# Weight units split in two halves by GpSimd, tensor tiles that wait half by half, four rows at the end of the first tiles, and two convolutions in another order

## The reference

```python
for l in range(2):
    x = layer_norm(ALPHA * x + 0.5 * swiglu(x, ffn_w12[l, 0], ffn_w3[l, 0]), ...)
    x = layer_norm(ALPHA * x + hybrid_mixer(x, ...), ...)          # delta net, RG-LRU, band attention
    x = layer_norm(ALPHA * x + memory_cross_attention(x, mem, xa_wq[l], xa_wkv[l], xa_wo[l]), ...)
    x = layer_norm(ALPHA * x + 0.5 * swiglu(x, ffn_w12[l, 1], ffn_w3[l, 1]), ...)
```

## Time and profile before

| | us |
|---|---|
| median of 3 runs | 3212.9 |
| lowest and highest run | 3211.45, 3213.68 |
| time of the profiled execution | 3213.97 |
| its span, first to last instruction | 3212.1 |
| PE busy | 3122.7 (97%) |
| POOL busy | 1751.3 (55%) |
| DVE busy | 1485.7 (46%) |
| ACT busy | 713.5 (22%) |

### The profile page before, as it was taken

How to read it: one execution, slowest core, us unless ns; L and a number is a source line. 1 busy time by engine, 2 the same in 40 slices (tenths; PEclk the granted TensorE clock), 3 DMA queues, 4 the chain that set the end, 5 groups by cost and what they waited for, 6 DMA issues and landing times.

```text
span 3212.1 us, 44735 instructions
## 1 busy us (share of the span) xinstructions
PE 3122.7 (97%) x15968; PEld 2598.2 (81%) x15968; DVE 1485.7 (46%) x2218; ACT 713.5 (22%) x1433; POOL 1751.3 (55%) x1003
## 2 busy tenths in 40 slices
PE   8999999999999999999999999999999999999997
PEld 7888876788888878888888888667888888788886
DVE  4342357755536335332243314667565372353423
ACT  1110223422222223110121102244222122231102
POOL 6666553433346755666656675525333558466663
PEclk9999999999999999999999999999999999999998
DMA  4233221211122322323323233212111223222231
GB/s 152 93 98 104 97 92 40 73 56 57 53 79 86 112 79 86 98 94 102 99 87 98 98 100 101 79 47 73 53 53 54 91 86 119 72 86 97 93 104 60
DMA packets 81190, 272.94 MB, mean 85 GB/s; under 512 B 8432, under 2 KB 16912, under 8 KB 81040
## 3 DMA queue, kind: packets, MB, share of 16 engines
q1 hardware_dynamic: 75808, 264.27, 25.3%
q10 hardware_dynamic: 5088, 5.96, 0.6%
q0 software_dynamic: 144, 0.66, 0.1%
HBM read 268.73 MB, written 2.12 MB: 84 GB/s over the span
## 4 chain that ended last, share of the span: by engine, by line
PE 88%; DVE 4%; issue 4%; POOL 2%; ACT 1%; DMA 0%; DVEq 0%; ACTq 0%; POOLq 0%; SPq 0%
PE acc L613 76%; PE aux L613 11%; POOL wh L596 1%; POOL wl L598 1%; PE aux L874 1%; DVE ycl L1720 0%; DVE dc L1891 0%; ACT xf L1317 0%; DVE li L1950 0%; DVE xl L1720 0%; DVE xf L1799 0%; DVE lc L1951 0%; DMA raw<-in_stream 0%; ACT tmp L1317 0%; ACT xh L1317 0%
## 5 line engine op out<-in xcount | busy, mean ns | idle before, releaser
L596 POOL TENSOR_SCALAR wh<-raw 128x1024 fp32r<-128x1024 f32 x496 | 540.2, 1089 | 1378.9 <-PE acc L613 792.1
L598 POOL TENSOR_TENSOR wl<-raw,wh 128x1024 fp32r<-128x1024 f32 x496 | 1212.4, 2444 | 41.3
L613 PE MATMUL acc<-xh,wh 128*128 128x512 f32 (+1 forms) x2688 | 1016.2, 383 | 32.3 <-ACT xh L1317 14.7
L613 PE MATMUL acc<-xh,wl 128*128 128x512 f32 (+1 forms) x2688 | 986.4, 372 | 0.0
L613 PE MATMUL acc<-xl,wh 128*128 128x512 f32 (+1 forms) x2688 | 942.4, 372 | 0.0
L613 PEld LDWEIGHTS acc<-xh,wh 128*128 128x128 f32 x2688 | 514.3, 191 | 142.3 <-issue 39.4
L613 PEld LDWEIGHTS acc<-xh,wl 128*128 128x128 f32 x2688 | 514.6, 191 | 79.1 <-issue 1.9
L613 PEld LDWEIGHTS acc<-xl,wh 128*128 128x128 f32 x2688 | 487.1, 191 | 87.4
L1720 DVE TENSOR_TENSOR hl<-tmp,hh 128x512 f32 x88 | 236.9, 2692 | 81.9 <-ACT hh L1317 81.9
L613 PE MATMUL acc<-hl,wh 128*128 128x512 f32 (+1 forms) x704 | 264.5, 376 | 0.0
L613 PE MATMUL acc<-hh,wl 128*128 128x512 f32 (+1 forms) x704 | 264.5, 376 | 0.0
(11 more groups left out here) (286 smaller groups left out, 3924.1 us busy)
## 6 DMA issues: line engine op xcount, KB each, us to landing
raw<-in_stream SPq DMA_DIRECT2D x496, 512.0 KB, 3.3
xf<-in_xT SPq DMA_DIRECT2D x2, 1024.0 KB, 9.6
bias<-rel_scratch ACTq DMA_DIRECT2D x2, 1024.0 KB, 6.0
mraw<-in_memT ACTq DMA_DIRECT2D x2, 1024.0 KB, 6.0
out_xT<-xf SPq DMA_DIRECT2D x16, 128.0 KB, 1.7
gate_w<-in_gate_w ACTq DMA_DIRECT2D x2, 512.0 KB, 4.8
const<-in_const POOLq DMA_DIRECT2D x1, 640.0 KB, 7.4
sc<-in_ba_w ACTq DMA_DIRECT2D x2, 256.0 KB, 4.9
```

The lines of the kernel that those rows point to most:

```text
L596: pool.tensor_scalar(wh[:, s, :], raw[:, s, :], 1.0, 0.0, ALU.mult, ALU.add).then_inc(hi_step, 1)
L598: pool.tensor_tensor(wl[:, s, :], raw[:, s, :], wh[:, s, :].bitcast(F32), ALU.subtract).then_inc(unit_split, 1)
L613: return pe.matmul(out, w, x, start=start, stop=stop, skip_group_check=True)
```

## The change

1. **Halves.** `split` does a unit in two halves of 512 columns: high part, remainder, high part, remainder. `unit_split` and `hi_step` now count halves. SyncE's wait is doubled accordingly.
2. **Waits half by half.** `simple_tile` and `first_pairs` wait for the first half of the unit ahead of k = 0, and for the second ahead of k = 4. Every other user of a unit waits for both halves, as before.
3. **Four rows at the end.** `together` is `KD // 2` = 4 where it was 6.
4. **Start.** The transfers of the two halves of x are issued one unit later each.
5. **Banks.** `att_v` and `mem_v` wait for a bank ahead of that bank's first matmul.
6. **Convolutions.** For head 0, conv2 moves from level 2 behind `rate` in level 4; conv1 of head 1 moves from there behind silu2 in level 5.
7. **Merge.** `low_part` of the two earlier rows stands ahead of the drain of the next two.

```diff
@@ def dve_beside
-            2: only(n, "decay", "silu0", "conv2"), 4: [(n - 1, "rate")] + (only(1, "conv1") if n == 0 else []),
-            5: only(n, "k_normed", "silu2") + only(p, "z_gate"), 6: only(p, "o_normed", "y") + only(n, "q_normed")}.get(s, [])
+            2: only(n, "decay", "silu0") + (only(n, "conv2") if n else []),
+            4: [(n - 1, "rate")] + (only(0, "conv2") if n == 0 else []),
+            5: only(n, "k_normed", "silu2") + (only(1, "conv1") if n == 0 else []) + only(p, "z_gate"),
+            6: only(p, "o_normed", "y") + only(n, "q_normed")}.get(s, [])
...
@@ SyncE
-                if s < 2:
-                    sp.dma_start(xf[:, :, tokens(s)], x_rows[:, :, tokens(s)]).then_inc(x_loaded[s], 16)
+                if 1 <= s < 3:
+                    sp.dma_start(xf[:, :, tokens(s - 1)], x_rows[:, :, tokens(s - 1)]).then_inc(x_loaded[s - 1], 16)
...
-                    sp.wait_ge(unit_split, i * SLOTS + (s - SLOTS + 1))
+                    sp.wait_ge(unit_split, i * (2 * SLOTS) + 2 * (s - SLOTS + 1))
...
@@ GpSimd
             def split(i, s):
-                pool.tensor_scalar(wh[:, s, :], raw[:, s, :], 1.0, 0.0, ALU.mult, ALU.add).then_inc(hi_step, 1)
-                pool.wait_ge(hi_step, i * SLOTS + (s + 1))
-                pool.tensor_tensor(wl[:, s, :], raw[:, s, :], wh[:, s, :].bitcast(F32), ALU.subtract).then_inc(unit_split, 1)
+                for m in range(2):
+                    c = slice(m * UNIT // 2, (m + 1) * UNIT // 2)
+                    pool.tensor_scalar(wh[:, s, c], raw[:, s, c], 1.0, 0.0, ALU.mult, ALU.add).then_inc(hi_step, 1)
+                    pool.wait_ge(hi_step, i * (2 * SLOTS) + (2 * s + m + 1))
+                    pool.tensor_tensor(wl[:, s, c], raw[:, s, c], wh[:, s, c].bitcast(F32), ALU.subtract).then_inc(unit_split, 1)
...
@@ TensorE
-                pe.wait_ge(unit_split, layer * UNITS + (u + 1))
+                pe.wait_ge(unit_split, 2 * (layer * UNITS + u + 1))
+
+            def half_unit_here(layer, u):
+                pe.wait_ge(unit_split, 2 * (layer * UNITS + u) + 1)
...
@@ first_halves, first_by_arrival
-                together = KD - 2
+                together = KD // 2
...
@@ attention
-                for t in range(CH):
-                    free_bank(l, "att_v", t - 3)
                 for n in range(4):
                     unit_here(l, UNIT0["att_v"] + n)
                     for t in range(CH):
+                        if n == 0:
+                            free_bank(l, "att_v", t - 3)
...
@@ VectorE, merge
                 for d in range(0, KD, 2):
-                    drain(l, PARTS_TO[INDEX["up", 0, d + 1]])
                     if d:
                         low_part(d - 2)
                         low_part(d - 1)
+                    drain(l, PARTS_TO[INDEX["up", 0, d + 1]])
                 low_part(KD - 2)
                 low_part(KD - 1)
```

More of the change, by code:

```diff
@@ L624, in unit_here, with unit @@
             def unit_here(layer, u):
-                pe.wait_ge(unit_split, layer * UNITS + (u + 1))
-            def unit(out, s, k_tiles, at, rhs, start, stop, ready=None, begins=True):
+                pe.wait_ge(unit_split, 2 * (layer * UNITS + u + 1))
+            def half_unit_here(layer, u):
+                pe.wait_ge(unit_split, 2 * (layer * UNITS + u) + 1)
+            def unit(out, s, k_tiles, at, rhs, start, stop, ready=None, begins=True, second_half=None):
                 for n, k in enumerate(k_tiles):
+                    if n == KD // 2 and second_half is not None:
+                        second_half()
                     low_ready = None if ready is None else ready(k)
@@ L653, in simple_tile @@
                 free_bank(l, name, i * 4 + (n - 3))
-                unit_here(l, i * 4 + (UNIT0[name] + n))
-                unit(acc[:, n % 4, cols], n % SLOTS, range(KD), 0, rhs, True, True, ready).then_inc(acc_ready.sem, 1)
+                u = i * 4 + (UNIT0[name] + n)
+                half_unit_here(l, u)
+                unit(acc[:, n % 4, cols], n % SLOTS, range(KD), 0, rhs, True, True, ready,
+                     second_half=lambda: unit_here(l, u)).then_inc(acc_ready.sem, 1)
             def normed(l, norm, half=None):
@@ L674, in first_pairs @@
                         if k == 0 and half != 1:
+                            half_unit_here(l, UNIT0[name] + n)
+                        if k == KD // 2 and half != 1:
                             unit_here(l, UNIT0[name] + n)
@@ L1181, in memory_values @@
             def memory_values(l, k):
-                if k == 0:
-                    for t in range(4):
-                        free_bank(l, "mem_v", t - 3)
                 unit_here(l, UNIT0["mem_v"] + k)
                 for t in range(4):
+                    if k == 0:
+                        free_bank(l, "mem_v", t - 3)
                     tok = slice((t // 2) * P, (t // 2 + 1) * P)
@@ L2069, in beside @@
                         silu_of(n, 0)
-                        head_conv(l, n, 2)
+                        if n:
+                            head_conv(l, n, 2)
                     if s == 4:
@@ L2074, in beside @@
                         if n == 0:
-                            head_conv(l, 1, 1)
+                            head_conv(l, 0, 2)
                     if s == 5:
@@ L2080, in beside @@
                             silu_of(n, 2)
+                            if n == 0:
+                                head_conv(l, 1, 1)
                         if p >= 0:
```

## The result

| us | before | after |
|---|---|---|
| median (runs) | 3212.74 (4) | 3192.78 (4) |
| lowest and highest run | 3211.45, 3213.68 | 3189.86, 3192.90 |
| profiled execution, and its span | 3213.97, 3212.1 | 3192.75, 3191.0 |

The ratio is 0.9936, with a 95% interval of 0.9919 to 0.9953: 20 us faster, and 0.2 us from the forecast of 3193. The sum was met; several of its terms were not, and their errors in part cancelled.

A forecast was written before the change was run, and what follows sets the result against it. PE was taken as the bound, busy 3122.7 of 3212.1 us, leaving some 90 us of idle time, and low-clock time, to win. Terms (b) to (i) sum to -20.0, taking 3212.9 to 3192.9 us; range 3183 to 3204.

The forecast's parts named there:

- (b): First tiles of three later FFNs: PE's stops for GpSimd's split units go, -5.6 us; x arriving later costs +0.5.
- (c): Kernel start: first matmul later, at 11.35, then no 2.57 us stop and an earlier clock rise; -4.3 us.
- (d): Delta net, wait for `rates`: without conv2 ahead of the reciprocal on VectorE, PE resumes 2.7 us earlier per layer, -5.3.
- (e): Delta net behind the `rates` stop: half of the 3.4 us low-clock stretch's cost counted as gained, -1.7 us for two layers.
- (f): `att_v`: first matmul no longer waits for the preceding tile's eviction, -2.1 us; `mem_v` 0.
- (g): Merge: remainders of the earlier rows are made in an idle stretch, so PE waits less; -3.7 us for both layers.
- (h): Cross attention, `mem_k` and `mem_v`: GpSimd is the bound; dearer units less an earlier start cost +3.1 us per layer, +6.2.
- (i): Seven layer norms: GpSimd's shorter instructions block VectorE less, 0.6 us at each place, -4 us (0 to -8).
- (a): GpSimd's splitting: halves add 0.33 us a unit, 3.50 to 3.83 us; bounds 0.16 and 0.82.
- the rival of the low clock: Fewer stops keep the clock up ahead of layer norms' ends, about half of seven 1.7 us stretches; 3183 us, 10%.
- the signs that I had named as making the prediction wrong: Unit over 4.0 us; new PE stops at k=4 in plain tiles; first tiles' tile 0 waiting for x over 0.3 us.

The follow-up runs named there:

- the shift: Changed kernel plus seven 512-column matmuls behind the very first tiles, their result unused, adding 1.6 us of work: 3193.78 us, ratio 0.9941.

## Why the prediction was right, step by step

| term | forecast | measured |
|---|---|---|
| (b) stops for `wl` at three FFNs, and reserve of x | -5.1 | -5.3 |
| (c) start | -4.3 | -4.8 |
| (d) `rates` | -5.3 | -6.1 |
| (e) clock | -1.7 | -3.3, at other places |
| (f) banks | -2.1 | -2.1 |
| (g) merge | -3.7 | -4.0 |
| (h) cross attention | +6.2 | +9.1 |
| (i) less blocking, at norms | -4 | -2.9 |
| less blocking in the delta nets, not forecast | | -1.9 |
| all else | | +0.3 |
| sum | -20.0 | -21.0 |

The measured terms come from the stretches above. Where a stretch holds two causes, I gave the clock 1.65 us for each place of low clock less (the pairs of kernels say 1.5 to 1.6, so up to 0.15 too much for each), the stop for `wl` its loss from start to start, and the rest to the blocking; the 0.2 that lack to 21.2 are rounding.

That -20.0 and -21.0 lie so close is in part luck. (h) came out 2.9 us dearer than forecast and (i) at the norms 1.1 smaller, while (e) gave 1.6 more, at places that I had not named, and the delta nets 1.9 that I had not forecast at all. The mechanisms of (b), (f) and (g) held, and that of (h) with too small a price.

**(a) Price of a half, and (h): right mechanism, too small.** 0.43 us instead of 0.33. The step that failed is the fixed cost of an instruction, taken as 0.14 for the high part and 0.11 for the remainder; the three widths give 0.19 to 0.20 and 0.15 to 0.18. The estimate from the Trainium skill (GPSIMD Engine Reference, section 3.1), 0.39, was nearer. (Two slips in the working change nothing: twice the slope of the memsets is 1.74 ns a column, not 1.78, and 0.39 a unit makes 8.1 us, not 8.2.) Each layer pays 6.5 us in the stretch and gets 2.0 from the earlier start ahead of it. The run with whole units there confirms it from the other side.

**(b) First tiles of the later FFNs: right.** All three stops for `wl` are gone, with 1.7 to 1.9 us each. The experiments give the credit to the four rows; the halves alone would nearly have done it too (31.48 us with whole units, 31.69 with the halves alone, 31.39 with both).

**(c) Start: right.** -4.8 for -4.3. The first matmul came at 11.21 (forecast 11.35), and the clock rose at 15.0 (forecast 16.3), so the loop began at 36.13 instead of 36.6. Two things limit that. The rise is not fixed by the code. Five kernels whose first tiles are issued alike (the changed one, whole units in the cross attention, all units whole, the old order of convolutions, the shift) made their first matmul at 11.0 to 11.2, and their clocks rose at 15.0, 16.8, 16.5, 14.2 and 16.7; so some 0.8 us of this term is chance. And the halves, to which I gave the end of the 2.57 us stop, are not needed for it: with whole units the start took 36.54 and PE did not stop, with halves alone, in the old order of transfers, 38.84 with stops of 1.07 and 0.84.

**(d) `rates`: the size was right, the reason only in part.** The order alone gives 2.70 us a layer (with whole units), which is the 2.7 that I forecast for it; but the halves alone give 3.06, and both together 3.06. In the changed kernel with the old order the halves give 2.23: how much depends on which of VectorE's instructions a subtraction meets (4.58 us for the conv there, 3.46 in the kernel with halves alone). I had taken the length of VectorE's work in the earlier trace rows as fixed, and so booked all of this under the order, while it was GpSimd that stretched it. Two edits with one effect were taken for one.

**(e) Clock behind that wait: wrong in place.** It stayed low there, in both layers. Four other places are gone: one at the first layer norm and one in the first delta net, worth 1.65 us each, and two in the first tiles of `ffn_up1`, worth nothing. In those PE, now 1.5 us earlier, waits for x instead:

```profile
1228.34 0.39 PE L617 MATMUL acc<-xh,wh 128*128 128x256 f32 x1 [1.17 <-ACT xh L1329]
```

The kernel with all units whole has the low clock there and no such wait, and the same length (31.48 against 31.39). So the rival of the low clock (3183) did not come: places went, and half of them gave nothing.

**(f) Banks: right,** 22.40 to 21.35, -2.1 for -2.1. All seven kernels with the new bank waits had 21.35, and the one without them (halves alone) 22.40.

**(g) Merge: right,** -4.0 for -3.7. In layer 0 the stretch took 8.33 us before, 8.16 with the halves alone, 7.22 with the new place of `low_part` and whole units, and 6.35 with both: here two edits need each other, and the sum had counted them as one.

**(i) Less blocking: the blocking is real, its worth came in part elsewhere.** The waits for `y_sum` fell by 6.4 us. Whether that shortens a norm depends on the next wait, the one for `xh`. In layer 1, the `att_qk` stretch took 42.54 us before and 42.52 after: the 1.70 for `y_sum` are gone and the wait for `xh` went from 0.55 to 2.16, so PE waits as long in all, only later. At `att_qk` of layer 0 and `ffn_up0` of layer 1 the same 1.7 went, the wait for `xh` grew only from 2.17 to 2.38 and from 2.05 to 2.18, and the gain was kept (in 35.74 to 32.28 the stop for `wl` is the other half). Why the norms differ was not followed up. The Trainium skill (SBUF — State Buffer, "Who interferes with whom") says that such instructions exclude each other for a whole instruction; the means of 2692, 1273 and 917 ns agree as far as they go, since the instruction gets shorter as GpSimd's does.

Of the signs that I had named as making the prediction wrong, one came: PE stops at k = 4 inside plain tiles, twelve times 0.21 us, all in `mem_k`. It was a bad sign to name. GpSimd is the bound there, as (h) says, and a consumer that waits half by half behind it has to stop at each half; the stretch ends with GpSimd's sixteenth unit either way, and in the FFN loop, where the sign would have told something, no such stop shows. The other two did not come: a unit costs 3.93 us, under the 4.0, and tile 0 of `first_rows` does not wait for x; the waits for `xh` stand ahead of it, in the pairs of the first half of the tokens.

## What to carry to other kernels

When a producer on GpSimd works ahead, split its units only where a consumer waits for the first part or where VectorE is on the critical path; where GpSimd sets the pace, leave them whole (here 7.4 us more). Look at the start by itself too: quarters lost 4.9 us there. When several edits aim at one wait, ask of each what it gives without the others: the order of convolutions and the halves removed the same 3 us a layer, four rows at the end made the half waits at the FFN heads needless, and the order of the first transfers made them needless at the start. And list the stretches of low clock before giving a gain of a few microseconds to an edit, in more than one execution if you can.

## What the runs showed of the hardware that I had not expected

The same stop is followed by the low clock in one run and not in another. The first rows are of the changed kernel, the second of the one with whole units in the cross attention, both at the first layer norm, behind the same matmuls and the same idle time:

```profile
384.48 0.39 PE L617 MATMUL acc<-xh,wh 128*128 128x256 f32 x1 [2.38 <-ACT xh L1329]
384.70 0.28 PE L617 MATMUL acc<-xh,wl 128*128 128x256 f32 x1
```
```profile
385.33 0.47 PE L625 MATMUL acc<-xh,wh 128*128 128x256 f32 x1 [2.38 <-ACT xh L1337]
385.60 0.42 PE L625 MATMUL acc<-xh,wl 128*128 128x256 f32 x1
```

They stand 0.85 us later in the second run; the difference ahead of them that I found is the clock's first rise, at 16.8 us instead of 15.0. The kernels had 13, 9, 11, 11, 11, 9, 5, 9 and 7 such places (before, after, and the experiments in the order above), worth some 9 to 10 us between before and the halves alone, 0.3%: about as much as the largest edits here. Many follow no stop at all: in every kernel one stands in the middle of each delta net, with no stop of PE in the 7 us ahead. What decides their number was not settled; the kernel has a part in it, since the kernel before had 0.990 or 0.991 in each execution and five of six with halves alone 0.994 or 0.995, and so has the single execution.

The second surprise is how far a GpSimd instruction reaches into VectorE's time: VectorE's work of 1485.7 us fell to 1288.8 with halves and 1189.7 with quarters, at the same instructions. Not only remainders are stretched by it, but also the three-operand instructions of the convolutions (5.14 to 3.46 us for three) and the `decay` product (2.88 to 0.68).
